# First adaLN modulation with the weight quarters stationary in TensorE, and reordered loads, in a three-block fp32 kernel

## The reference

```python
act_lat = jax.nn.silu(c)
act_ctx = jax.nn.silu(c_ctx)
sh_l, sc_l, gt_l = split(act_lat @ w_ada[0] + b_ada[0], 3)
u_lat = rms_norm(x, norm_g[0]) * (1.0 + sc_l) + sh_l
sh_c, sc_c, gt_c = split(act_ctx @ w_ada[0] + b_ada[0], 3)
u_ctx = rms_norm(ctx, norm_g[0]) * (1.0 + sc_c) + sh_c
p_lat = u_lat @ w_in
```

## Time and profile before

| | |
|---|---|
| median of 3 runs | 1381.28 us (1381.2 to 1383.26) |
| the profiled execution | 1380.69 us |
| its span | 1378.9 us |
| TensorE (PE) busy | 1347.4 us, 98% |
| PE weight loads (PEld) busy | 1121.8 us, 81% |
| DVE / ACT / POOL busy | 749.2 / 567.7 / 503.4 us |
| loaded from HBM | 130.51 MB |

### The profile page before, as it was taken

How to read it: one execution, slowest core, us unless ns; L and a number is a source line. 1 busy time by engine, 2 the same in 40 slices (tenths; PEclk the granted TensorE clock), 3 DMA queues, 4 the chain that set the end, 5 groups by cost and what they waited for, 6 DMA issues and landing times.

```text
span 1378.9 us, 18100 instructions
## 1 busy us (share of the span) xinstructions
PE 1347.4 (98%) x6881; PEld 1121.8 (81%) x6881; DVE 749.2 (54%) x1014; ACT 567.7 (41%) x888; POOL 503.4 (37%) x235
## 2 busy tenths in 40 slices
PE   8999999999999999999999999999999999999998
PEld 4688788789988888877779889788888888888886
DVE  3685888864845437567538346245437244253442
ACT  3453555533533354445545344342344132241331
POOL 0243011146532393412224333244555444444441
PEclk9999999999999999999999999999999999999999
DMA  9872001175331142311133222233333333333331
GB/s 343 283 231 70 9 22 31 31 254 163 92 92 46 43 156 77 107 43 46 39 87 93 62 76 76 61 92 92 92 92 108 94 105 91 93 105 91 95 104 62
DMA packets 206582, 136.05 MB, mean 99 GB/s; under 512 B 10137, under 2 KB 187914, under 8 KB 206522
## 3 DMA queue, kind: packets, MB, share of 16 engines
q1 hardware_dynamic: 206320, 135.18, 32.4%
q10 hardware_dynamic: 202, 0.06, 0.0%
HBM read 130.51 MB, written 4.72 MB: 98 GB/s over the span
## 4 chain that ended last, share of the span: by engine, by line
PE 86%; DVE 7%; ACT 2%; DMA 2%; issue 1%; POOL 1%; SPq 0%; ACTq 0%; DVEq 0%; POOLq 0%
PE psum L2049 28%; PE psum L2050 27%; PE psum L2051 27%; DMA ada_w<-in_w_ada 2%; DVE pt_lo L1541 1%; PE psum L2097 1%; PE psum L2246 1%; DVE neg_max L1548 1%; PE psum L2488 1%; ACT pt_hi L922 1%; DVE probs L1536 1%; POOL w_lo L666 1%; PE psum L2612 1%; PE psum L2186 0%; ACT w_hi L776 0%
## 5 line engine op out<-in xcount | busy, mean ns | idle before, releaser
L666 POOL TENSOR_TENSOR w_lo<-w_raw,w_hi 128x1024 fp32r<-128x1024 f32 x180 | 441.6, 2458 | 699.1 <-ACT w_hi L776 571.0
L2049 PE MATMUL psum<-u_hi,w_hi 128*128 128x512 f32 (+1 forms) x960 | 369.0, 384 | 2.7 <-POOL w_lo L666 2.1
L2050 PE MATMUL psum<-u_lo,w_hi 128*128 128x512 f32 (+1 forms) x960 | 361.4, 376 | 0.0
L2051 PE MATMUL psum<-u_hi,w_lo 128*128 128x512 f32 (+1 forms) x960 | 361.3, 376 | 0.0
L776 ACT ACTIVATE w_hi<-w_raw 128x1024 fp32r<-128x1024 f32 x180 | 189.3, 1056 | 206.0 <-PE psum L2051 154.9
L2049 PEld LDWEIGHTS psum<-u_hi,w_hi 128*128 128x128 f32 x960 | 181.5, 189 | 39.9 <-POOL w_lo L666 2.5
L2051 PEld LDWEIGHTS psum<-u_hi,w_lo 128*128 128x128 f32 x960 | 181.4, 189 | 33.6
L2050 PEld LDWEIGHTS psum<-u_lo,w_hi 128*128 128x128 f32 x960 | 181.6, 189 | 31.8 <-issue 0.7
L2049 PE MATMUL psum<-y_hi,w_hi 128*128 128x512 f32 x416 | 162.4, 390 | 0.0
L2050 PE MATMUL psum<-y_lo,w_hi 128*128 128x512 f32 x416 | 161.9, 389 | 0.0
L2051 PE MATMUL psum<-y_hi,w_lo 128*128 128x512 f32 x416 | 161.9, 389 | 0.0
(11 more groups left out here) (456 smaller groups left out, 2279.5 us busy)
## 6 DMA issues: line engine op xcount, KB each, us to landing
w_raw<-in_w_in SPq DMA_DIRECT2D x52, 512.0 KB, 3.8
w_raw<-in_w_up SPq DMA_DIRECT2D x32, 512.0 KB, 4.0
w_raw<-in_w_down SPq DMA_DIRECT2D x32, 512.0 KB, 3.6
ada_back<-in_w_ada SPq DMA_DIRECT2D x7, 2048.0 KB, 10.4
ada_w<-in_w_ada SPq DMA_DIRECT2D x4, 2048.0 KB, 14.8
w_raw<-in_fno_w_in SPq DMA_DIRECT2D x16, 512.0 KB, 3.7
w_raw<-in_mla_w_in SPq DMA_DIRECT2D x11, 512.0 KB, 5.2
w_raw<-in_mla_w_out SPq DMA_DIRECT2D x8, 512.0 KB, 3.8
```

Source lines behind the costliest of these rows:

```text
L666: pool.tensor_tensor(WL[:, j, :], RAW[:, j % 2, :], f(WH[:, j, :]), ALU.subtract).then_inc(lo_done, 1)
L2049: pe.matmul(out, ah, bh, start=first, stop=False)
L2050: pe.matmul(out, ah, bl, start=False, stop=False)
L2051: return pe.matmul(out, al, bh, start=False, stop=last)
```

## The change

- `ada(q)` is turned round: a 128 x 128 block of the quarter is stationary, and the two columns of `c_act` move. 8 x 4 matmuls of 2 columns leave the result in columns at once. All four quarters go this way; `weigh_quarter`, `last_columns`, `turn_row` and the ACT row copies are gone.
- TensorE's order is now: quarter 0, bias table, 16 fillers, first half of quarter 2, spread of 1/rms, second half of quarter 2, chunks 0 and 1 of tiles 0 and 1, quarter 1, chunks 2 and 3, quarter 3, chunks 0 to 3 of tile 2, chunks 4 to 7 of tiles 0 and 1, the rest of tile 2, tile 3 with the context transposes.
- `x` and quarter 0 are loaded in two halves each. The transposes of `x` begin on the first half. The order of loads is tile 0, quarter 2, tile 1, quarter 1, tile 2, quarter 3, context, key tile. The second `gate_load` now also waits for three finished quarters.
- The mask is a 33rd row of the bias product, where it was added by DVE from a 128 x 640 tile; DVE only copies the result.
- ACT splits tile 2 right after the first four chunks of `u_hi`, ahead of the context's work.

```diff
             sp.dma_start(IDENT[:], d["identity"]).then_inc(s_const, 16)
-            sp.dma_start(XTOK[:], d["x"].rearrange("(m p) n -> p m n", p=P)).then_inc(s_x, 16)
-            sp.dma_start(AQ[0][:], ada_weights(0)).then_inc(s_adaq[0], 16)
...
-            for q in range(1, 4):
-                sp.dma_start(AQ[q][:], ada_weights(q)).then_inc(s_adaq[q], 16)
+            for n in range(2):
+                sp.dma_start(XTOK[:, 2 * n:2 * n + 2, :], d["x"][2 * P * n:2 * P * (n + 1), :].rearrange("(m p) n -> p m n", p=P)).then_inc(s_x[n], 16)
+            for n, loaded in enumerate((s_adaq[0], s_first)):
+                sp.dma_start(AQ[0][:, 4 * n:4 * n + 4, :], ada_weights(0)[:, 4 * n:4 * n + 4, :]).then_inc(loaded, 16)
...
             sp.wait_ge(row_ss, TT + 1)
             sp.wait_ge(x_t, KC)
+            sp.wait_ge(ada_mm, 3)
             gate_load(1)
...
-            ada_row_copy(0, 0, 1)
-            ada_row_copy(1, 2, 2)
-            split_hi(A0, None, 0)
-            split_hi(A0, None, 1)
+            for j in range(2):
+                split_hi(A0, None, j)
             for c in range(4):
                 lat_hi(c)
-            ada_row_copy(2, 3, 4)
+            split_hi(A0, None, 2)
...
-            v.wait_ge(s_adaq[1], 16)
-            v.wait_ge(cact_done, 2)
-            weigh_quarter(0)
+            v.wait_ge(bias_mm, 1)
+            v.tensor_copy(BROW[:], PB[:, 0:TOEP]).then_inc(bias_row, 1)
             v.wait_ge(row_ss, TT + 1)
...
-            weigh_quarter(1).then_inc(ada_used, 1)
-            v.wait_ge(bias_mm, 1)
-            v.tensor_tensor(BROW[:], PB[:, 0:TOEP], MROW[:], ALU.add).then_inc(bias_row, 1)
...
                 for k in range(k0, k1):
-                    mm = pe.matmul(ada_row_bank(q)[0:2, :], CACT[:, k, :], AQ[q][:, k, :], start=k == 0, stop=k == KC - 1)
+                    if q == 0 and k == 4:
+                        pe.wait_ge(s_first, 16)
+                    for b in range(4):
+                        mm = pe.matmul(ada_columns(q)[:, 2 * b:2 * b + 2], AQ[q][:, k, b * P:(b + 1) * P], CACT[:, k, :],
+                                       start=k == 0 and b == 0, stop=k == KC - 1 and b == 3)
...
-            turn_row(0, 0)
-            for _ in range(8):
-                pe.matmul(bank(3, P), ONES[:], ONES[:], start=True, stop=True)
-            ada(2)
+            for _ in range(16):
+                pe.matmul(bank(6, P), ONES[:], ONES[:], start=True, stop=True)
+            ada(2, 0, 4)
             pe.wait_ge(diag_done, TT)
...
-            ada(3, 0, 1)
-            turn_row(1, 2).then_inc(ada_mm, 1)
-            ada(3, 1, KC)
+            ada(2, 4, KC)
...
+            lat_steps(0, 2)
+            pe.wait_ge(mod_done, 1)
+            ada(1)
+            lat_steps(2, 4)
+            ada(3)
+            pe.wait_ge(lo_done, 3)
+            for k in range(4):
+                lat_step(2, k)
+            lat_steps(4, KC)
+            for k in range(4, KC):
+                lat_step(2, k)
+            pe.wait_ge(lo_done, 4)
             for k in range(KC):
...
+                lat_step(3, k)
+                turn_ctx(k)
```

More of the change, by code:

```diff
@@ L432, in turned_ctx @@
             return bank(6 + c % 2, TC)
-        ADA0 = 5
-        def ada_row_bank(q):
-            return bank(2 if q == 3 else 6)
+        ADA0 = 4
         def ada_columns(q):
@@ L535, in gate_tile @@
                 load_tile(G1 + r - r % 4, None, r % 4, d["mla_w_in"][:, c0:c0 + P], KC)
+            sp.dma_start(T5[:], d["t5_bias_2"]).then_inc(s_t5, 16)
+            sp.dma_start(HOT[0:BUCKETS, :], d["bucket_hot"]).then_inc(s_t5, 16)
+            sp.dma_start(HOT[BUCKETS:BUCKETS + 1, :], d["mask_row"][0:1, :]).then_inc(s_t5, 16)
             load_tile(A0, None, 0, d["mla_w_in"][:, 0:P], KC)
+            sp.dma_start(AQ[2][:], ada_weights(2)).then_inc(s_adaq[2], 16)
             load_tile(A0, None, 1, d["mla_w_in"][:, P:2 * P], KC)
+            sp.dma_start(AQ[1][:], ada_weights(1)).then_inc(s_adaq[1], 16)
+            load_tile(A0, None, 2, d["mla_w_in"][:, 2 * P:3 * P], KC)
+            sp.dma_start(AQ[3][:], ada_weights(3)).then_inc(s_adaq[3], 16)
             sp.dma_start(CTOK[:], d["ctx"].rearrange("(m p) n -> p m n", p=P)).then_inc(s_ctx, 16)
+            key_rope_tile()
             sp.dma_start(COS[:], d["rope_cos"]).then_inc(s_mask, 16)
@@ L800, in _ @@
                 x_copy(c)
-            act.wait_ge(s_x, 16)
+            act.wait_ge(s_x[0], 16)
+            act.wait_ge(s_x[1], 16)
             for m in range(TT):
@@ L1378, in _ @@
             v.wait_ge(s_t5, 48)
-            v.tensor_copy(T5R[:].rearrange("b (h a) -> b h a", h=MH), T5[:].unsqueeze(2).to_broadcast([BUCKETS, MH, P // MH]))\
+            v.memset(T5R[BUCKETS:BUCKETS + 1, :], 1.0).then_inc(bias_row, 1)
+            v.tensor_copy(T5R[0:BUCKETS, :].rearrange("b (h a) -> b h a", h=MH), T5[:].unsqueeze(2).to_broadcast([BUCKETS, MH, P // MH]))\
                 .then_inc(bias_row, 1)
[L1382 to L1390, removed]
-            v.wait_ge(s_adaq[1], 16)
-            v.wait_ge(cact_done, 2)
-            weigh_quarter(0)
+            v.wait_ge(bias_mm, 1)
+            v.tensor_copy(BROW[:], PB[:, 0:TOEP]).then_inc(bias_row, 1)
             v.wait_ge(row_ss, TT + 1)
@@ L1428, in _ @@
             for half in range(2):
-                v.wait_ge(ada_mm, ADA0 if half else 3)
+                v.wait_ge(ada_mm, ADA0 if half else 2)
                 if half == 0:
@@ L2075, in _, with turn_x @@
             pe.wait_ge(s_const, 16)
-            pe.wait_ge(s_x, 16)
-            def turn_x(c):
+            def turn_x(c, m0, m1):
                 if c >= 6:
                     pe.wait_ge(x_copied, c - 5)
-                for m in range(TT):
+                for m in range(m0, m1):
                     mm = pe.transpose(bank(c % 6, P, m * P), XTOK[:, m, c * P:(c + 1) * P], IDENT[:])
-                mm.then_inc(x_t, 1)
-            for c in range(5):
-                turn_x(c)
+                if m1 == TT:
+                    mm.then_inc(x_t, 1)
+            pe.wait_ge(s_x[0], 16)
+            for c in range(6):
+                turn_x(c, 0, 2)
+            pe.wait_ge(s_x[1], 16)
+            for c in range(4):
+                turn_x(c, 2, TT)
             pe.wait_ge(s_vec, 16 * (len(VECS) + 2))
             pe.transpose(bank(7, NROWS), VROWS[:], IDENT[0:NROWS, 0:NROWS]).then_inc(cols_t, 1)
-            for c in range(5, KC):
-                turn_x(c)
+            for c in range(4, 6):
+                turn_x(c, 2, TT)
+            for c in range(6, KC):
+                turn_x(c, 0, TT)
             def ada(q, k0=0, k1=KC):
@@ L2145, in lat_step, with lat_steps @@
                 return three(bank(j), wsl(WH, j, k), wsl(WL, j, k), UH[:, k, :], UL[:, k, :], k == 0, k == KC - 1)
-            pe.wait_ge(lo_done, 2)
-            pe.wait_ge(bias_row, 2)
-            for k in range(KC):
[L2150 to L2163, removed]
+            def lat_steps(k0, k1):
+                for k in range(k0, k1):
+                    pe.wait_ge(u0_lo, k + 1)
+                    for j in range(2):
+                        mm = lat_step(j, k)
+                        if k == KC - 1:
+                            mm.then_inc(tile_done, 1)
+            pe.wait_ge(lo_done, 2)
+            pe.wait_ge(bias_row, 3)
+            lat_steps(0, 2)
[10 more added lines that the diff above has]
+            pe.wait_ge(lo_done, 4)
+            for k in range(KC):
+                lat_step(3, k)
+                turn_ctx(k)
             for j in range(2, 4):
```

48 lines of the change are left out of this document (14 added, 34 removed).

## The result

| | before | after |
|---|---|---|
| median | 1381.24 us (4 runs, 1380.87 to 1383.26) | 1407.53 us (4 runs, 1402.27 to 1410.14) |
| profiled execution, its span | 1380.69, 1378.9 | 1408.36, 1406.5 |
| mean granted clock of TensorE | 0.994 | 0.974 |
| tile 3 done (first `uc_hi` product) | 72.24 | 99.90 |

The ratio is 1.0182 [1.0164, 1.0200]: slower by 26 us. The forecast was 1385.8 with a range up to 1391.5; the time lies outside it, near the 1407 that the clock rival gave for half clock throughout.

A forecast was written before the change was run, and what follows sets the result against it. TensorE, busy 98% of the span, was taken to bound the kernel. The opening's +3.2 us plus +1.3 for the clock made +4.5: 1380.69 became 1385.2, and 0.6 more for the median gave 1385.8 us; 8-in-10 range 1381.8 to 1391.5.

The forecast's parts named there:

- the clock rival: Two-column quarters: TensorE's clock falls there; 1391 with one half-speed stretch per quarter, 1407 throughout; chance 0.13.
- the clock: Opening, at the 3.4 us stop: one half-speed stretch of 3.3 us, taken at +1.3 us.
- The sum: Opening up to tile 3's end, step by step: 75.4 against 72.24, +3.2 us without the clock.
- light end: Two-column quarters: one half-speed stretch in each of three on the path, 5.1 us above the forecast, 1391.
- the 1.9 us of that form: Old trace, 45.7 to 47.6: two-column passes at full clock, cited against a clock fall in such passes.
- second modulation: After first latent passes and quarters 1 and 3: reached at 56.3, against 47.52 before.
- The turned roles save nothing in TensorE: Quarters: 64 passes at 0.112 make 7.2 us, against 7.03 for the old second quarter.
- No cover for the chain: Before the first latent step: nothing queued under the modulation chain, so TensorE stands still for 3.4 us.
- The second modulation chain: After quarter 3: tile 2's first half (2.8) covers most of the 3.4 us chain, leaving 0.6 idle.
- The old stop of 2.13: TensorE's wait before tile 3, at 59.45 in the old kernel: shrinks to about 0.1 us.
- Does a weight load follow the clock?: Two-column passes: assumed to slow at half clock, as 0.22 against 0.112 us; the 107 ns estimate would cost about 0.7.
- The end of the span follows tile 3: Opening's end at 72.24: whatever tile 3's end gains or loses there is the result.

The follow-up runs named there:

- padded kernel: Changed kernel with the two condition columns padded to 128 moving columns in all four quarters; 1385.2 us, ratio 1.0021. Also written "128 columns".
- the filled stop: Changed kernel with 128 moving columns, plus 14 filler matmuls in the stop before the first latent product; 1383.65 us, ratio 1.0017.
- padded kernels: Changed kernel with 128 moving columns, with 64, and with 128 and the stop filled: 1385.2, 1384.71 and 1383.65 us.
- row form of the change: Changed kernel's loads, order and fillers, but quarters as before: condition vectors stationary, 512 columns moving, rows copied by ACT and turned; 1388.46 us, ratio 1.0049.
- first version that beats both: Changed kernel with quarters in the old row form, 0, 2, 3, 1 back to back, no fillers; 1377.91 us, ratio 0.9973 to the kernel before.

## Why the prediction was wrong

**The step that failed** is the clock. The sum gave it +1.3 us for one stretch behind the stop; four stretches came, 57.7 us in all, and each began inside a quarter of two-column passes. The measured loss is about 25 us (99.90 - 75.4 = 24.5, or 47% of 54.3). The rival "the clock falls in the two-column stretches" had 0.13, and the range took in its light end only. Against it I had put the 1.9 us of that form that stayed at full clock in the old trace. That row was too short to bear this: in the change, too, the first 2.5 to 4.2 us of every such stretch were at full clock, and the fall came behind them. The row could not tell "stays" from "falls later", and I used it as if it could. With that row saying so little, the chance should have been nearer to that of the forecast, and the range should have reached to 1407.

**Point by point.** The padded kernel shows how the sum fares when the clock holds in the quarters; the changed kernel shows what the clock did to it.

| step | forecast | 128 columns | after |
|---|---|---|---|
| quarter of 64 passes | 7.2 | 7.3 | 9.8, 11.3, 10.6 (quarters 0, 1, 3) |
| quarter 0 starts | 12.6 | 12.75 | 12.52 |
| quarter 2 starts | 24.6 | 24.94 | 31.06 |
| stop before the first latent product | 3.4 | 3.58 | 3.45 |
| first latent product | 36.3 | 36.72 | 47.42 |
| second modulation | 56.3 (58.0 with one stretch) | 58.10 | 78.8 |
| tile 3 done | 75.4 (77.1) | 77.67 | 99.90 |

- *Start, filler, quarter 2, the stop, the order*: right, each within 0.5 us in the padded kernel. "The turned roles save nothing in TensorE" holds at full clock.
- *No cover for the chain*: right; 3.45 us of idle. The stretch behind it is real and costs about 1.6 (the filled stop). In the change the clock was down already, so the stop added no loss of clock there.
- *The second modulation chain*: 0.6 idle forecast, 0.76 in the padded kernel, none in the change, where slow TensorE passes covered it. The old stop of 2.13 before tile 3 was to shrink to 0.1; no such stop is in either timeline.
- *The price of the rival*: 1407 came, but not as it was worked out, and that the number fits is luck. The rival doubled three quarters, 21.6 us. A pass of 2 columns at half clock took 0.213, not 0.224, and parts of each quarter were at full clock, so the three quarters (2, 1 and 3) lost 4.0 + 4.1 + 3.4 = 11.5. The other half fell on work the rival had left out: quarter 0 (2.6), table (1.2), fillers (2.7), the spread of 1/rms (0.9), latent passes (some 6). A clock that falls in one row stays down for its neighbours.
- *Does a weight load follow the clock?* In the forecast the row at half clock stood against the 107 ns of the Trainium skill ("TensorE: Matmul & The Clock Gate", section "LDWEIGHTS (loading the stationary operand)"). The row was right: 6.83 / 32 = 0.213 a pass at half clock with 2 columns moving, against 0.113 at full clock, and weight loads fill that row (from 37.2 to 43.9 they are busy 6.68 of 6.70 us).
- *The end of the span follows tile 3*: right, 27.6 of 27.7. For the padded kernels the opening says +5.4, +4.7 and +3.7 and the medians +3.0, +2.5 and +1.5. This sets the opening of one profiled execution of the kernel before, of 1380.69 us, against medians of it above 1382. Between the profiled spans alone the padded kernels are +4.1, +3.1 and +3.8 (1383.0, 1382.0 and 1382.7 against 1378.9), so at most 1.6 us of the opening's delay came back, and nothing in the third; whether that is more than the spread between runs was not tried.

## What to carry to other kernels

When a change keeps TensorE's busy time but makes it move few columns for each weight load, price it at half clock from a few microseconds in (2.5 to 4.2 here), and what follows it too, until a trace of equal length shows otherwise; a short row at full clock is no such trace. Read the granted clock beside every busy share, as 98% busy was true of both kernels. A stop can be paid twice, once as idle and once as a slow stretch: the stops of 3.4 to 3.6 us before the first latent product all had half clock inside or behind them, unless fillers ran in them. So put independent work under a chain that ends in another engine.

## What was not expected of the hardware

- Passes with 128x128 weights took 0.112 to 0.114 us with 2, 64 and 128 moving columns at full clock, and widening from 2 to 128 columns made the kernel 22 us faster.
- Weight loads without a gap did not bring the clock back: from 54.3 to 63.1 of the changed kernel they are busy 8.80 of 8.80 us, with no DMA traffic beside, all at half clock.
- The same stop does not always lower the clock: 2.13 us for the low part of tile 3 was followed by full clock in the old kernel and by a half-speed stretch in the old kernel with 128-column passes added. Before quarter 2, a stop of 2.82 us was followed by one in the kernel with 2-column passes added (28.7), and a stop of 2.92 us in the kernel with 128-column passes by none (clock 1.00 from 20 to 44). Why was not tried.
- Four small DVE operations that overlap one of POOL took 2.99 us, 2.32 with 128 columns padded and 3.02 in the row form of the change; where POOL was idle they took 0.88 in the old kernel, and 0.87 in the change without fillers and in the first version that beats both. TensorE's timeline shows no wait for them. DVE's row, then POOL's, of the changed kernel:

```profile
25.79 2.99 DVE L1373 TENSOR_SCALAR rstd_diag<-ident,row_rstd 128x128 f32<-128x128 f32 x4
...
26.34 2.36 POOL L662 TENSOR_TENSOR w_lo<-w_raw,w_hi 128x1024 fp32r<-128x1024 f32 x1 [2.82 <-ACT w_hi L772]
```
